# Expert rows gathered as quarter rows and turned in 32 by 32 blocks on VectorE instead of on TensorE

## The reference

```python
def expert_choice_ffn(h, w_router, w_gate, w_up, w_down):     # called for each sequence
    t = h.reshape(N, D)                                       # D = 1024, N = 272 and 1040
    cap = CAPACITY_FACTOR * N // N_EXPERTS                    # 34 and 130 rows, 16 experts
    aff = softmax(t @ w_router, axis=-1)
    gate, idx = lax.top_k(aff.T, cap)                         # each expert picks its rows
    xe = t[idx]
    hid = silu(xe @ w_gate) * (xe @ w_up)
    ye = (hid @ w_down) * gate[..., None]
    out = zeros((N, D)).at[idx].add(ye)                       # rows may be picked more than once
    return out
# x = x + expert_choice_ffn(rmsnorm(x)); the output is rmsnorm(x)
```

## Time and profile before

| | us |
|---|---|
| median of 3 runs | 1757.08 |
| lowest and highest | 1756.59, 1758.20 |
| profiled execution, its own time | 1759.55 |
| its span, from the first to the last instruction | 1757.6 |

### The profile page before, as it was taken

The page is one execution under the profiler, slowest core; times in us unless marked ns, Lnnn a source line. Parts: engine busy times, 40 slices in busy tenths (PEclk is TensorE's granted clock), DMA queues, the critical chain, the costliest instruction groups (busy, mean ns, idle before and its releaser), DMA issues.

```text
span 1757.6 us, 24801 instructions
## 1 busy us (share of the span) xinstructions
PE 1727.0 (98%) x10305; PEld 1400.0 (80%) x10305; DVE 422.0 (24%) x987; ACT 382.6 (22%) x890; POOL 298.6 (17%) x330
## 2 busy tenths in 40 slices
PE   9999999999999999999999999999999999999996
PEld 6555556855555774456999999999999999999996
DVE  5562113621020660079101101011010110101105
ACT  3334224332121534464000000000000000000005
POOL 0080022520101354342010010100101001010010
PEclk9999999999999999999999999999999999999998
DMA  9211013321110536433668676876768758597585
GB/s 305 72 52 60 13 36 80 87 90 36 37 49 12 169 92 218 143 114 141 225 235 289 227 245 228 278 272 217 258 226 303 253 201 283 203 313 258 181 284 220
DMA packets 179192, 307.92 MB, mean 175 GB/s; under 512 B 11244, under 2 KB 65052, under 8 KB 178960
## 3 DMA queue, kind: packets, MB, share of 16 engines
q1 hardware_dynamic: 171840, 283.30, 47.3%
q0 software_dynamic: 7248, 23.09, 5.3%
HBM read 275.02 MB, written 31.35 MB: 174 GB/s over the span
## 4 chain that ended last, share of the span: by engine, by line
PE 92%; DVE 5%; ACT 1%; issue 1%; DMA 1%; POOL 0%; SPq 0%; DVEq 0%; ACTq 0%; POOLq 0%
PE bank L2134 32%; PE bank L2154 16%; PE bank L1905 12%; PE bank L1882 9%; PE bank L2036 5%; PE bank L1816 3%; PE bank L1852 2%; PE bank L1966 2%; PE bank L1947 1%; DVE arena L1576 1%; DVE arena L1574 1%; DVE arena L1578 1%; PE bank L1862 1%; PE bank L1860 1%; PE bank L2178 1%; PE bank L2109 1%
## 5 line engine op out<-in xcount | busy, mean ns | idle before, releaser
L2134 PE MATMUL bank<-arena 128*128 128x164 f32 x4096 | 581.4, 303 | 0.3 <-DVE arena L1673 0.3
L2134 PEld LDWEIGHTS bank<-arena 128*128 128x128 f32 x4096 | 573.5, 190 | 0.5 <-DVE arena L1673 0.5
L2154 PE MATMUL bank<-arena 128*128 128x164 f32 x2048 | 296.4, 303 | 0.4 <-DVE arena L1684 0.4
L2154 PEld LDWEIGHTS bank<-arena 128*128 128x128 f32 x2048 | 286.7, 190 | 0.6 <-DVE arena L1684 0.6
L1905 PE MATMUL bank<-arena 128*128 128x512 f32 (+1 forms) x576 | 214.1, 534 | 0.0
L1905 PEld LDWEIGHTS bank<-arena 128*128 128x128 f32 x576 | 109.8, 191 | 103.1 <-issue 92.9
L1684 DVE TENSOR_TENSOR arena<-bank,arena 128x328 f32<-128x328 f32 x64 | 32.0, 500 | 657.5 <-ACT arena L1254 657.5
L833 POOL DMA_INDIRECT residual<-arena,cur_scatter x30 | 44.9, 1498 | 691.7 <-DVE arena L1693 633.2
L1882 PE MATMUL bank<-arena 128*128 128x384 f32 x480 | 155.7, 485 | 0.0
L1254 ACT ACTIVATE arena<-bank 128x328 f32<-128x328 f32 x64 | 28.4, 444 | 559.6 <-PE bank L2134 559.6
L2036 PE MATMUL bank<-arena 128*128 128x512 f32 x320 | 146.1, 599 | 0.8 <-issue 0.7
(11 more groups left out here) (273 smaller groups left out, 1501.5 us busy)
## 6 DMA issues: line engine op xcount, KB each, us to landing
arena<-in_w_up SPq DMA_DIRECT2D x32, 2048.0 KB, 15.3
arena<-in_w_down SPq DMA_DIRECT2D x32, 2048.0 KB, 9.9
arena<-in_w_gate SPq DMA_DIRECT2D x32, 2048.0 KB, 8.4
arena<-in_w_in SPq DMA_DIRECT2D x7, 1536.0 KB, 6.5
arena<-in_x_sample SPq DMA_DIRECT2D x14, 512.0 KB, 6.6
arena<-x_features_first SPq DMA_DIRECT2D x11, 512.0 KB, 8.6
arena<-decay_rows SPq DMA_DIRECT2D x22, 256.0 KB, 4.6
arena<-state_rows SPq DMA_DIRECT2D x44, 128.0 KB, 4.1
```

The lines of the kernel that those rows point to most:

```text
L2134: last = pe.matmul(ps[2 * w + fp % 2][:, a * SLOTS:(a + 1) * SLOTS], ring[2 * (fp // 2) + w][:, k, f * P:(f + 1) * P], xeT[:, k, SIDE[side ...
L2154: last = pe.matmul(to, ring[4 + dp // 2][:, k, dt * P:(dt + 1) * P], hidT[:, k, :], start=k == 0, stop=k == KT - 1)
```

## The change

Each row of 1024 features is taken as four quarter rows of 256. A gather now fetches 128 quarter rows: the four quarters of 32 picked rows, quarter q on partitions 32q to 32q + 31. Six such gathers (`GROUPS`) make one expert, 192 slots (`SLOT_W`), of which 28 are spare and carry row numbers past the last real row and the gate value 0. One VectorE instruction turns all 32 by 32 blocks of this into `xeT` (`turn_rows`), and four turn the results out of the banks of the down product into `yeq` (`turn_results`), 192 columns each. ScalarE multiplies the quarter rows by the gate values in place (`gate_rows_of`), and GpSimd adds them in six additions that don't wait for one another. The order of features that results from the blocks is taken up by the weights, whose rows (gate, up) and columns (down) are reordered on the host ahead of the launch. Experts are no longer paired. TensorE's order for experts 1 to 14 becomes a hardware loop as well.

Row numbers and gate values are laid out fourfold by VectorE, transposed by TensorE into bank 6 (12 transposes of 16 partitions by 128, behind the first gate and up group), and read out as `idx_q` (4 x row number + quarter) and `gate_q`. Expert 0's rows and expert 15's results are still transposed on TensorE.

```diff
+GROUPS = -(-SLOTS // 32)
+SLOT_W = 32 * GROUPS
+QUARTER = D // 4
 ...
# GpSimd
-                def gather(j, n_steps):
-                    pool.tensor_copy(cur_gather[:, 0, :], idxc[:, 0, bass.ds(j * 2, 1)]).then_inc(idx_step, 1)
 ...
-                    for blk, n in ((0, P), (1, TAILS), (2, P)):
-                        pool.indirect_dma_start(out=xe[0:n, blk, :], out_offset=None, in_=t_d[:, :],
-                                                in_offset=bass.IndirectOffsetOnAxis(ap=cur_gather[0:n, blk, :], axis=0)).then_inc(xe_in, 16)
+                def gather(e, n_steps):
+                    pool.tensor_copy(cur_gather[:, :], idx_q[:, bass.ds(e * GROUPS, GROUPS)]).then_inc(idx_step, 1)
 ...
+                    for g in range(GROUPS):
+                        pool.indirect_dma_start(out=xeq[:, g * QUARTER:(g + 1) * QUARTER], out_offset=None, in_=t_quarters[:, :],
+                                                in_offset=bass.IndirectOffsetOnAxis(ap=cur_gather[:, g:g + 1], axis=0)).then_inc(quarters_in, 16)
+                def scatter(e, n_steps):
 ...
+                    for g in range(GROUPS):
+                        pool.wait_ge(gated, e * GROUPS + g + 1)
+                        pool.sem_inc(passed, 1)
+                        pool.indirect_dma_start(out=acc_quarters[:, :], out_offset=bass.IndirectOffsetOnAxis(ap=cur_scatter[:, g:g + 1], axis=0),
+                                                in_=yeq[:, g * QUARTER:(g + 1) * QUARTER], in_offset=None, compute_op=ALU.add).then_inc(acc_out, 16)
+                    pool.wait_ge(acc_out, e * 16 * GROUPS + 16 * GROUPS)
 ...
+                gather(1, 0)
+                with pool.Fori(0, NE - 2) as i:
+                    pool.wait_ge(rows_turned, i + 1)
+                    gather(i + 2, i * 2 + 1)
+                    scatter(i, i * 2 + 2)
# ScalarE
+                def gate_rows_of(e):
+                    act.wait_ge(dn_done, e * 4 + 6)
+                    for g in range(GROUPS):
+                        rows = yeq[:, g * QUARTER:(g + 1) * QUARTER]
+                        act.activation(rows, rows, ACT.Copy, scale=gate_q[:, bass.ds(e * GROUPS + g, 1)]).then_inc(gated, 1)
+                with act.Fori(0, NE - 1) as i:
+                    silu(i)
+                    gate_rows_of(i)
# VectorE
+                def turn_rows(e):
+                    dve.wait_ge(quarters_in, e * 16 * GROUPS)
+                    dve.transpose(xeT.rearrange("p k (g s) -> p g k s", g=GROUPS),
+                                  xeq.rearrange("p (g k s) -> p g k s", g=GROUPS, k=KT)).then_inc(rows_turned, 1)
+                def turn_results(e, dp):
+                    if dp == 0:
+                        dve.wait_ge(ye_free, e + 1)
+                    dve.wait_ge(dn_full, e * 4 + dp + 1)
+                    dve.transpose(yeq.rearrange("p (g k s) -> p k g s", g=GROUPS, k=KT)[:, 2 * dp:2 * dp + 2, :, :],
+                                  result_tiles(4 + dp % 2).rearrange("p f (g s) -> p f g s", g=GROUPS)).then_inc(dn_done, 1)
+                with dve.Fori(0, NE - 1) as i:
                     for m in range(4):
+                        hidden(i, m)
+                    turn_rows(i + 1)
                     for m in range(4):
+                        turn_results(i, m)
# TensorE
                 for fp in range(4):
-                    gate_up(0, None, fp, 4)
-                    if fp == 0:
-                        pe.wait_ge(xe_in, 32)
-                    transpose_first(4 + fp)
+                    gate_up(0, fp, True)
+                    if fp == 0:
+                        quarter_ranked()
-                for i in range(PAIRS - 1):
+                with pe.Fori(0, NE - 2) as i:
 ...
+                        down(i, m)
                     for m in range(4):
+                        gate_up(i + 1, m)
```

308 lines of the change are left out of this document (123 added, 185 removed).

## The result

The changed kernel takes 1717.84 us (median of 4 runs, 1716.59 to 1718.89) against 1757.64 us for the kernel before (4 runs, 1756.59 to 1759.14): a ratio of 0.9773, with a 95% interval of 0.9756 to 0.979. It is 39.8 us faster; 1719.0 was forecast. The profiled execution took 1716.59 us, its span 1714.8.

What follows compares the result with a forecast made beforehand. TensorE, busy for 98% of the span, was taken as the bound. -38.3 + 1.1 - 0.9 = -38.1 us from the median 1757.08 gave 1719.0 us; own range 1716.5 to 1724, 8 in 10 within 1716 to 1740.

Steps and rivals of the forecast that it cites:

- part 1: TensorE no longer does transposes in the loop, for expert 14's results and in expert 0's groups: 38.3 us removed.
- Part 2: 12 row-number transposes on TensorE behind the first gate and up group add 1.1 us; VectorE's fourfold copies cost nothing.
- Part 3: Start: expert 0's last gather has 36 rows instead of 100, so the first product starts 0 to 1.2 us earlier; 0.9 taken.
- Part 4: New work of VectorE, ScalarE and GpSimd in each expert fits their slack: cost 0.
- Part 5: DMA engines with 1 KB gathered and added packets reach 79%, not a bound; upper end 126%.
- Part 6: TensorE's code becomes a loop of 14 passes with 13 jumps back, 0 to some 3 us a jump; 0 taken.
- The rival: TensorE's 13 jumps fetch code, about 3 us each plus one at entry, 42 us in all: 1761 us; chance 0.08.
- Part 7: End: expert 14's additions land 16.4 us behind its down product, before the tiles are read: cost 0.

Runs made afterwards that it cites:

- transposes_back: Changed kernel with 6 idle 128 by 128 transposes on TensorE behind each gate and up group of the loop, 24 per expert: 1755.29 us.
- tail100: Changed kernel with 100 rows instead of 36 in the one gather of expert 0's tail, the added ones read by nobody: 1720.69 us.
- turn4: Changed kernel with VectorE turning the next expert's rows 4 times instead of once, the extra turns into memory nobody reads: 1718.6 us.
- turn6: Changed kernel with VectorE turning the next expert's rows 6 times instead of once: 1785.8 us.
- gathers3: Changed kernel with each of an expert's six gathers issued three times back to back, the extra ones into memory nobody reads: 1918.68 us.
- body3: Changed kernel with three experts in one pass of TensorE's loop (about 2360 instructions), 4 passes, last two experts written out: 1723.29 us, one run.
- wait_at_3: Changed kernel with the down product waiting for its last hidden product at its third matmul instead of its seventh: 1730.0 us.
- gathers3_apart: Changed kernel with 18 gathers per expert in three batches of six, each begun only when the six before have landed: 1723.38 us, one run.
- gathers3_small: Changed kernel with 18 gathers per expert back to back, the 12 extra ones of 8 rows each instead of 128: 1719.22 us, one run.

## Why the prediction was right, and where it was not

**What bounds, and part 1 (transposes leave TensorE, 38.3).** Right. 35.86 in the loop for 35.6, 1.76 for 1.8, and the last three groups of expert 0's gate and up product are 0.55 us shorter, of some 0.66. transposes_back shows it from the other side.

**Part 2 (12 transposes, 1.1).** 0.84 us, on the path as said. The two fourfold copies took 0.66 us each instead of up to 1.1, in VectorE's idle time.

**Part 3 (the start, 0 to 1.2, taken as 0.9).** Mis-sized: 1.72 us. Of this 0.34 us lie ahead of the first rows' transposes (they begin 6.09 us behind the row numbers instead of 6.43), a place that the term did not count. The bound of 1.2 came from counting VectorE's read-outs one behind another at the durations of the kernel before. They were 1.29 us for the two whole ones and now 1.72 for all four. The term also left out what TensorE does after the wait: its idle time before the first group shrank from 1.26 and 0.33 us to 0.55, and the clock no longer fell (1.00, before 0.84): the first group's products take 9.10 us instead of 10.69 (845.03 to 855.72), 1.59 us more. tail100 ties both to the gather. That is most of the difference between the forecast and the result.

**Part 4 (VectorE, ScalarE, GpSimd: 0).** Right in every place. The block transposes are cheaper than their estimates (1.77 for 2.3 us, 0.58 for 0.6). The slack at the seventh matmul is 0.5 us, as forecast; turn4 and turn6 put the point at which the turning of rows reaches TensorE between four and six times its price. The added scalings end at 899.85, 21.2 us behind the down product's start at 878.61 (21.0). Behind them ScalarE loads a table for 1.28 us in each expert (`ACT_TABLE_LOAD`, 14 times from 900 to 1600 us, and not once in that stretch before), which the part did not have; the next SiLU comes at 905.53, 4.4 us behind that load, so it costs nothing.

**Part 5 (DMA engines, 79%).** Right in the sum, off in its terms. 900 to 1600 us of the changed kernel:

```profile
q1 hardware_dynamic: 81983, 165.34, 65.5%
q0 software_dynamic: 15121, 20.59, 15.0%
```

80.5% in all. The added 1 KB packets took 102 ns in the median and 119 in the mean, where 83 was taken. The gathered rows are not in the trace as 768 packets of 1 KB, but as 192 of 4 KB at 176 ns, which is less than 768 x 53 would be. What the part did not ask is how many gathers may follow one another without a pause; that had no row in the trace before, and gathers3 shows that it would have decided had the change asked for three times as many.

**Part 6 (TensorE's loop, 0 to 3 us a jump, taken as 0).** 0, and the reason given (fetches never showed) was only half of it: there were no fetches, as the code packets fell from 82 to 39. The rival had the right mechanism for a body three times as long, and too high a price, 3 us for 2.2: 13 such jumps would have cost 29 us and left a gain of 11.

**Part 7 (the end).** Right. The additions of expert 14 have landed when SyncE reads the tiles at 1659.70, 15.1 us behind the end of that down product at 1644.58, where 16.4 was forecast. The longest wait left for TensorE in the last expert was there before, as long (1724.74, 0.36 us):

```profile
1682.40 1.80 PE L2152 MATMUL bank<-arena 128*128 128x164 f32 x11 [0.36 <-DVE arena L1685]
```

**The sum.** -38.1 was forecast. By the table it is -40.9, and of the 2.8 us between them part 3 has 0.8 and its clock 1.6. The medians are 39.8 us apart, 1.7 from the forecast. The stated range reaches down to 1716.5, but its two reasons (0.3 us at the start, 0.4 us for the wait) add up to 1718.3 only, and the wait stayed. The result of 1717.84 is inside the stated range only because that was wider than its reasons: the start went beyond its bound, and the clock had no term in the sum.

## What to carry to other kernels

Where one engine is busy for 98% of the time, work that it shares with others is worth its full price on that engine and nothing on those with slack, even if it is dearer there; count the slack up to the first thing that the bound engine wants back, and check it with an experiment that multiplies the new work. An idle time of TensorE can have a second price behind it, the lower clock of the next group, and that belongs in the sum when a wait is added or removed: 1.6 to 1.8 us behind 2.61 and 4.36 us in the loop and behind 1.26 and 0.33 us at the start, nothing behind 1.13 to 1.70 us in body3. Put a wait between batches of indirect transfers before adding more of them: it cost 6.3 us once, in expert 0, and nothing after that, while 18 gathers without it held the other engines for 13 us in each expert.

## What the hardware showed unexpectedly

- Gathers of 128 rows (1 KB each) from GpSimd back to back hold the instruction streams of the other engines, ScalarE's and VectorE's from the seventh or eighth gather on and TensorE's from the eleventh: one instruction of TensorE every 0.70 us, for 13 us an expert, while the DMA engines are at 0.68. The bytes under way were no more than in the changed kernel, which has no hold.
- TensorE runs a loop of about 1570 instructions without fetching code again, and with about 2360 it fetches at each jump, which costs 1.4 to 2.8 us.
- After a gap of 2.61 us, and after 1.26 + 0.33 or 1.30 us, the next 64 records took 10.8 us (clock 0.84) instead of 9.1; after gaps of 0.5 us they did not, nor after 1.13, 1.70 and 1.32 us at the jumps of body3, where TensorE had run without a gap before. The length of the last gap alone does not decide.
- Part of the differences between traces lies in TensorE's filler transposes ahead of expert 0's rows. In eight of the twelve traces with the gather of 36 rows the first product starts 8.3 to 8.6 us behind the first transpose of the row numbers; in the other four (turn6, wait_at_3, gathers3_apart, gathers3_small) the 44 fillers take 1.6 us longer, at a lower clock (0.74 against 1.00), and it starts 9.9 us behind. The fillers in the changed kernel, then in gathers3_small:

```profile
834.62 5.18 PE L2002 MATMUL bank<-ident 128*128 128x128 f32 x44
```
```profile
836.21 6.81 PE L2008 MATMUL bank<-ident 128*128 128x128 f32 x44
```
